# Seven-product chunks with one up-projection tile in their middle, and conditioning and mixer panels at other places, in a two-block transformer kernel

## The reference

```python
def sq_relu_mlp(h, w_up, w_down):
    return jnp.square(jax.nn.relu(h @ w_up)) @ w_down          # w_up 1024 x 4096

for layer in range(2):
    h = rms_norm(x, norm_mix_g[layer])
    x = x + (fox_mixer(h, ...) if layer == 0 else mla_mixer(h, ...))
    x = x + sq_relu_mlp(rms_norm(x, norm_ffn_g[layer]), ffn_w_up[layer], ffn_w_down[layer])
```

## Time and profile before

| | us |
|---|---|
| median of 3 runs | 1981.91 |
| lowest, highest | 1981.55, 1983.43 |
| the profiled execution | 1981.71 |
| its span | 1980.0 |
| PE busy | 1961.3 |
| DVE busy | 1341.7 |
| ACT busy | 894.3 |

### The profile page before, as it was taken

The page is one execution under the profiler, slowest core; times in us unless marked ns, Lnnn a source line. Parts: engine busy times, 40 slices in busy tenths (PEclk is TensorE's granted clock), DMA queues, the critical chain, the costliest instruction groups (busy, mean ns, idle before and its releaser), DMA issues.

```text
span 1980.0 us, 29280 instructions
## 1 busy us (share of the span) xinstructions
PE 1961.3 (99%) x10404; PEld 1640.2 (83%) x10404; DVE 1341.7 (68%) x2145; ACT 894.3 (45%) x1417; POOL 60.4 (3%) x114
## 2 busy tenths in 40 slices
PE   9999999999999999999999999999999999999999
PEld 7777789898987887898988788778888888888888
DVE  6555579687777776797787769574444686563545
ACT  4555554445444554544444443474333544432333
POOL 0000000000110110000001100000000000000000
PEclk9999999999999999999999999999999999999999
DMA  4332243323562114523226513211322412223232
GB/s 158 86 85 85 75 148 129 106 79 98 184 205 78 52 49 157 179 69 106 96 99 214 190 46 104 74 64 65 96 96 98 151 43 85 96 95 105 88 99 91
DMA packets 61292, 209.05 MB, mean 106 GB/s; under 512 B 7160, under 2 KB 10232, under 8 KB 61200
## 3 DMA queue, kind: packets, MB, share of 16 engines
q1 hardware_dynamic: 49920, 168.32, 25.8%
q0 software_dynamic: 10560, 37.28, 6.0%
q10 hardware_dynamic: 720, 2.23, 0.3%
HBM read 205.66 MB, written 2.13 MB: 105 GB/s over the span
## 4 chain that ended last, share of the span: by engine, by line
PE 94%; DVE 4%; ACT 1%; DMA 1%; issue 1%; SPq 0%; DVEq 0%; ACTq 0%
PE bank L893 23%; PE bank L895 23%; PE bank L894 23%; PE bank L1216 4%; PE bank L1218 4%; PE bank L1217 4%; PE bank L1016 1%; PE bank L1091 1%; PE bank L1075 1%; PE bank L998 1%; PE bank L1001 1%; PE bank L1043 1%; PE bank L949 1%; PE bank L951 1%; PE bank L950 1%
## 5 line engine op out<-in xcount | busy, mean ns | idle before, releaser
L893 PE MATMUL bank<-b_hi,w_hi 128*128 128x512 f32 x2060 | 813.0, 395 | 6.6 <-DVE w_lo L2764 4.0
L895 PE MATMUL bank<-b_hi,w_lo 128*128 128x512 f32 x2060 | 802.9, 390 | 0.0
L894 PE MATMUL bank<-b_lo,w_hi 128*128 128x512 f32 x2060 | 802.7, 390 | 0.0
L893 PEld LDWEIGHTS bank<-b_hi,w_hi 128*128 128x128 f32 x2060 | 387.2, 188 | 95.9 <-issue 8.2
L895 PEld LDWEIGHTS bank<-b_hi,w_lo 128*128 128x128 f32 x2060 | 387.0, 188 | 81.0
L894 PEld LDWEIGHTS bank<-b_lo,w_hi 128*128 128x128 f32 x2060 | 387.4, 188 | 80.2 <-issue 2.4
L2764 DVE TENSOR_TENSOR w_lo<-w_raw,w_hi 128x1024 fp32r<-128x1024 f32 (+3 forms) x259 | 306.8, 1185 | 210.2 <-ACT w_hi L1810 209.5
L1810 ACT ACTIVATE w_hi<-w_raw 128x1024 fp32r<-128x1024 f32 (+3 forms) x259 | 265.5, 1025 | 263.3 <-PE bank L895 253.6
L3916 DVE SCALAR_TENSOR_TENSOR arena<-bank,vec,arena 128x511 f32<-128x511 f32 x88 | 65.7, 749 | 85.8 <-ACT arena L2658 80.5
L1216 PE MATMUL bank<-parts,w_hi 128*128 128x256 f32 x384 | 108.7, 283 | 3.3 <-DVE x L3113 3.3
L1218 PE MATMUL bank<-parts,w_lo 128*128 128x256 f32 x384 | 107.9, 281 | 0.0
...
## 6 DMA issues: line engine op xcount, KB each, us to landing
w_raw<-in_wstream SPq DMA_DIRECT2D x253, 512.0 KB, 3.5
arena<-in_ada POOLq DMA_DIRECT2D x48, 512.0 KB, 4.3
plain<-in_wseven SPq DMA_DIRECT2D x24, 512.0 KB, 5.0
early<-in_wseven SPq DMA_DIRECT2D x24, 512.0 KB, 6.8
...
x<-in_xT ACTq DMA_DIRECT2D x4, 512.0 KB, 6.6
```

What stands on the lines that cost most here:

```text
L893: nc.tensor.matmul(dst, whi, rhs_hi(k), start=(k == 0), stop=False)
L894: nc.tensor.matmul(dst, whi, rhs_lo(k), start=False, stop=False)
L895: last = nc.tensor.matmul(dst, wlo, rhs_hi(k), start=False, stop=(k == n - 1))
```

## The change

Within a chunk PE now makes products 0 to 13, then one up tile, the last that stood before the chunk, and then products 14 to 27. That tile's panel is split in two halves during products 10 to 12, and its eviction and its hidden-state work stand behind it. The chunk no longer waits for this tile at its start: product 0 waits for seven hidden tiles of its eight, product 1 for their sums, product 3 for the eighth. The set of sums goes from products 2 to 8 to products 16 to 22. Conditioning is dealt 6 + 12 + 6 in `ff_a` (two in each of the last six up tiles, the first six over five tiles), 3 in `mla_out`, and 6 + 12 + 3 in `ff_b`. The three mixer panels are split one by one in the down projection of `ff_b`, and both down projections are written out rather than looped, on ACT and DVE.

```diff
-        ADA_UP, ADA_POST = 9, 6
-        ADA_A = ADA_POST
+        ADA_EARLY, ADA_UP, ADA_POST = 6, 12, 6
+        ADA_A = ADA_EARLY
         ADA_MLA = ADA_A + ADA_UP + ADA_POST
-        ADA_MORE = ADA_MLA + ADA_POST
-        ADA_B = ADA_MORE + ADA_POST
+        ADA_MORE = ADA_MLA + 3
...
-            def seven_products(run, c):
-
-                pe.wait_ge(hid_lo, HID0[run] + (c + 1) * KT)
-                pe.wait_ge(mixed_low, MIXED_LOW0 + seven_first(run) + QUAD * (c + 1))
+            def seven_products(run, c, half):
+
+                if half == 0:
+                    pe.wait_ge(hid_lo, HID0[run] + (c + 1) * KT - 1)
...
+                n0 = QUAD * seven_chunk(run, c) + 2 * half
+                for n in range(n0, n0 + 2):
...
+                        if half == 0 and n == n0 and o == 1:
+                            pe.wait_ge(mixed_low, MIXED_LOW0 + seven_first(run) + QUAD * (c + 1))
+                        if half == 0 and n == n0 and o == 3:
+                            pe.wait_ge(hid_lo, HID0[run] + (c + 1) * KT)
...
-                    up_tiles(run, buf, first, n)
-                    first += n
                     if c < SEVEN_CHUNKS:
-                        seven_products(run, c)
+                        up_tiles(run, buf, first, n - 2)
+                        first += n
+                        tile(g0 + first - 2, t0 + first - 2, 0, buf)
+                        seven_products(run, c, 0)
+
+                        panel_ready(g0 + first - 1)
+                        bank_free(t0 + first - 1)
+                        products(acc[1][:], 0, KT, lambda k: b_hi[buf][:, k, :], lambda k: b_lo[buf][:, k, :], 0, P).then_inc(mm_done, 1)
+                        seven_products(run, c, 1)
+                    else:
+                        up_tiles(run, buf, first, n)
+                        first += n
                 for j in range(KT):
...
-                def up_tiles(first, n, c):
-                    for j in range(first, first + n):
-                        if j + 2 < first + n:
+                def up_tiles(first, last, c):
+                    i0 = SEVEN * QUAD * seven_chunk(run, c)
+                    for j in range(first, last):
+                        if j + 2 < last:
                             w_split(j + 2)
                         else:
                             act.wait_ge(mm_done, t0 + j + 1)
-                            for i in range(2):
-                                high(SEVEN * QUAD * seven_chunk(run, c) + 2 * (j + 2 - first - n) + i)
+                            high(i0 + 2 * (j + 2 - last))
                         square(j)
-                        if j % 2 and j < first + n - 1:
+                        if j + 2 >= last:
+                            high(i0 + 2 * (j + 2 - last) + 1)
+                        if j % 2:
                             sums_high(j // 2)
+
+                def chunk(c, last):
+
+                    end = SEVEN * QUAD
+                    at = end * seven_chunk(run, c)
+                    for i in range(end):
+                        act.wait_ge(seven_mm, MM0 + at + i + 1)
+                        if i + 4 < SEVEN_HALF or SEVEN_HALF <= i < end - 4:
+                            high(at + i + 4)
+                        elif i + 4 < SEVEN_HALF + 2:
+                            w_half(last, i + 4 - SEVEN_HALF, 0)
+                        elif i < SEVEN_HALF:
+                            high(at + i + 2)
+                        else:
+                            w_half(last + 1 + (i + 4 - end) // 2, i % 2, (i + 4 - end) // 2)
+                        if i == SEVEN_HALF - 1:
+                            act.wait_ge(mm_done, t0 + last + 1)
+                            high(at + SEVEN_HALF + 2)
+                            high(at + SEVEN_HALF + 3)
+                            square(last)
+                        if i == SEVEN_HALF + 6 and last // 2 < last_s:
+                            sums_high(last // 2)
 
                 w_split(0)
...
-                def last_square(j):
-                    square(j)
-                    if run == "ff_b":
-                        for p in range(MIX_W):
-                            mix_split(p)
-
-                segment(run, first + n, KT, last_mid, nothing, lambda: last_square(j), fresh=1)
-                return last_mid
+                def mid_split(k, s):
+
+                    last_mid(k, s)
+                    if run == "ff_b" and k % 2 and k < 2 * MIX_W:
+                        mix_split(k // 2)
+
+                segment(run, first + n, KT, mid_split, nothing, lambda: square(j), fresh=1, unrolled=True)
...
-                    if not (isinstance(j, int) and j >= ADA_POST):
-                        conditioning(j + j0, (s + j0) % 2, place)
+                    if not (isinstance(j, int) and not first <= j < ADA_POST):
+                        conditioning(j + (j0 - first), (s + j0 - first) % 2, place)
...
-                    at = (ADA_A if run == "ff_a" else ADA_B) + last_up + last_up // 2
-                    for i in range(at, at + 1 + last_up % 2):
+                    at = (ADA_A if run == "ff_a" else ADA_B) + 2 * last_up
+                    for i in range(at, at + 2):
                         conditioning(i, i % 2, 0 if run == "ff_a" else 1)
-                if 2 <= j < 2 + ADA_POST:
-                    i = (0 if run == "ff_a" else ADA_MORE) + j - 2
-                    conditioning(i, i % 2, 1)
+                if 2 <= j < 1 + ADA_EARLY:
+                    at = 0 if run == "ff_a" else ADA_MORE
+                    for i in range(at + j - 2 + (j > 3), at + j - 1 + (j > 2)):
+                        conditioning(i, i % 2, 1)
...
-                def up_tiles(first, n, c):
-                    for j in range(first, first + n):
-                        last = j == first + n - 1
+                def up_tiles(first, last, c):
+                    n0 = QUAD * seven_chunk(run, c)
+                    for j in range(first, last):
                         relu(j)
-                        if j % 2 == 0 and j > (first if c else 0):
+                        if j % 2 == 0 and j > (first if c else 0) and j + 1 < last:
                             sums_low(j // 2 - 1)
-                        if j + 2 < first + n:
+                        if j + 2 < last:
                             w_split(j + 2)
-                        elif last:
-                            low(SEVEN * QUAD * seven_chunk(run, c) + 2)
-                        else:
-                            n0 = QUAD * seven_chunk(run, c)
-                            two(n0)
+                        elif j + 2 == last:
                             low(SEVEN * n0)
+                            sums(j // 2)
                             low(SEVEN * n0 + 1)
                             three(n0)
-                        if not last:
-                            if j % 2:
-                                sums(j // 2)
+                            sums_low(j // 2)
+                        else:
+                            low(SEVEN * n0 + 2)
+                        if j + 2 < last and j % 2:
+                            sums(j // 2)
+                        if j + 1 < last:
                             hidden_low(j)
+                        if j + 3 == last:
+                            two(n0)
                         if c == 1 and j == first:
                             clear()
                             if run == "ff_b":
                                 first_conditions()
                         up_conditions(run, j)
+
+                def chunk(c, last):
+
+                    p, end = last // 2, SEVEN * QUAD
+                    mixes = p < last_s
+                    for i in range(end):
+                        at = end * seven_chunk(run, c) + i
+                        read(at)
+                        if i + 3 < SEVEN_HALF or SEVEN_HALF <= i < end - 3:
+                            low(at + 3)
+                        elif i + 3 < SEVEN_HALF + 2:
+                            w_half(last, i + 3 - SEVEN_HALF, 0, seven_count(at - i + SEVEN_HALF - 1))
+                        elif i < SEVEN_HALF:
+                            low(at + 1)
+                            low(at + 2)
+                            relu(last)
+                            low(at + 3)
+                        else:
+                            u = i + 3 - end
+                            w_half(last + 1 + u // 2, u % 2, u // 2, seven_count(at - i + end - 1) + u // 2)
+                        if i % SEVEN == 0:
+                            four(at // SEVEN)
+                        if i % SEVEN == 2 and i + 5 < end:
+                            two(at // SEVEN + 1)
+                        if i % SEVEN == 4 and i + 3 < end:
+                            three(at // SEVEN + 1)
+                        if i == 1:
+                            hidden_low(last - 1)
+                        if i == SEVEN_HALF + 1:
+                            hidden_low(last)
```

(24 more changed lines are left out.)

124 lines of the change are left out of this document (52 added, 72 removed).

## The result

The change is slower: 2002.76 us against 1982.67, a ratio of 1.0104 with a 95% interval of 1.0091 to 1.0116 (4 runs each). The forecast had the direction, +8.9 us, and missed the size: +20.1, outside the range.

What follows compares the result with a forecast made beforehand. PE, busy 1961.3 of 1980.0 us, was taken as the bound, losing time where DVE's queue lags; chunks 8.0 + ff_a 3.0 + ff_b 0.4 - mla_out 2.0 - loops 0.5 = +8.9, so 1990.8 us, range 1985.5 to 1996.5.

Steps and rivals of the forecast that it cites:

- Part 1, first half: Products before the middle tile: DVE's reads come late for PE, stalls of 1.45 + 1.05 + 1.05 = 3.55 us per run.
- the small ones: Chunks: some 0.05 us for each new restart of PE, 0.3 in a run.
- the product-4 wait: Chunk's first half: high(3) behind square makes low(3) and then read(2) 1.29 us late; PE stalls 0.9 at product 4.
- Parts 2 and 3: Middle tile's panel 0.2 us late, 0.65 a run; second half's old stall back at products 20 and 25, -0.45 a run.
- part 6: Unrolled down projections: PE's small gaps at loop steps go, -0.5 us (0 to -1); SP's chunk weight loads wait as before.
- Part 4, ff_a: Last up tiles: conditioning pairs 6.14 us apart against tiles of 5.44 make the first addition 3.3 late; +3.0 us.
- Part 4, ff_b: Tail: 5.0 us of new waits, no clock fall, against 4.6 that falls away; +0.4 us (-0.5 to +2.7).
- the rival to which I gave 0.12: The clock falls again behind a wait near 3 us, once or twice: +1.7 to +3.4 on top, 1994; chance 0.12.
- Part 5, mla_out: Three conditioning steps removed from mla_out end PE's late starts for an addition and a panel; -2.0 us (-1.5 to -2.2).

Runs made afterwards that it cites:

- highs_first: The change, with ACT's high(3) put ahead of the square of the last tile before a chunk, as before the change; 1997.3 us.
- first_seven_between: The change, with only the first group of seven's loads put between the last two panel loads ahead of a chunk; 1995.2 us.
- relu_later: first_seven_between and highs_first together, plus the middle tile's relu behind read(14), its low part and sums later, `four` during the middle tile; 1986.4 us.
- deal_mixed: deal_as_before, but with three conditioning steps in mla_out and twelve in ff_b's last up tiles; 1981.9 us, ratio 0.9998.
- mixers_alone: The kernel before, with only the mixer panels split one by one in ff_b's down projection and both down projections written out; 1977.9 us, ratio 0.9979.
- deal_as_before: relu_later with conditioning dealt as before: nine steps in each run's last up tiles, six in mla_out; 1977.0 us, ratio 0.9972.

## Why the prediction was wrong

- **The gap.** In the profiled execution it is 21.2 for 8.9: 6.3 for late weights, 0.5 for the rest of the chunks, 3.4 for ff_a's tail, 2.8 for ff_b's, less 0.3 for the loops and 0.4 ahead of chunk 0.
- **Part 1, first half**, 3.55 a run: right in its mechanism. Without late weights the late starts of the first halves sum to 4.0 and 3.8 in the two runs, with the small ones for which 0.3 was added, and highs_first took the product-4 wait away. **Parts 2 and 3**: the middle tile cost 0.22 (said 0.2), product 20 came back at 0.98 (said 1.0). In all 8.5 measured against 8.0, in first_seven_between.
- **The step that failed** is in part 6: "SP's loads of chunk weights wait as before, and their cover is the product time of a whole group of seven". That holds for groups 1 to 3 of a chunk. The first group's cover was the 15 us between its loads and `two` [before: 296.69 and 311.85], and I had costed `two` as work and not asked what it waits for. It is 6.3 us of the chunks' 14.8 (14.8 less 8.5). The fall of the clock in b0 is no part of it.
- **Part 4, ff_a**, +3.0: measured 6.4 (ff_a end +3.6, with the 2.0 of mla_out and the 0.8 of the loops put back). The spacing was right (6.11 for 6.14; 6.25 to 6.45 in the others' ff_a), two things were missing. The first pair began 2.9 late, its blocks not having landed; and I priced a pair at 2.28, while its second step waits for its own block (0.6 in the sixth pair of the change, 1.0 in relu_later's). Without the late first pair twelve steps for nine cost 5.1 (ff_a end, relu_later against deal_mixed), so 3.0 was too low by itself. By the Trainium skill's fit (DMA: Bandwidth & Descriptors, section Anatomy of one DMA) a load takes an estimate of 3.2 us and pairs are never late. The spacing of 6.11, less the 1.52 from step to issue, is 4.6 and speaks against it here.
- **Part 4, ff_b**, +0.4: measured +3.2. The late starts are 5.7 (start to start) where I had 5.0, and the clock fell all the same, 1.7 for the nothing that I had; what is left are pauses of 0.1 behind such starts. That what falls away is worth some 4.6 was right: mixers_alone has neither the wait nor the stretch, and is only 3.0 shorter because small late starts came in their place, of which the larger, 1.0, is not in the change. The fall was the rival to which I gave 0.12, but I had put it behind waits near 3 us. In the change it came behind two of the three waits of 1.8 and more (1.80 and 1.85, not 1.90).
- **Part 5, mla_out**, -2.0: right, 2.0 (deal_as_before and deal_mixed). **Part 6, loops** -0.5: ff_a end -0.8 in mixers_alone.
- **The range.** It took the bounds of each term (the lower ones add to +4.2 and not +4.4, and its low end is +3.6), but the bounds of a load's landing went only into the conditioning. The scatter of landings moves whole chunks by 1.8 us between kernels of equal code in them.

What stays open: why these loads had landed only 7.9 to 8.6 us after the first issue, where the median of the page is 5.1 a load, and which other transfer each of them meets.
